# Attention scores of a diffusion backbone from rounded queries and keys: one float32 product becomes three

## The chip, the cores and the metric

The program runs on one core of a Trainium2 chip. The metric is the device time of one execution in microseconds (us), the median of several runs. TensorE multiplies matrices, VectorE and ScalarE work elementwise, GpSimd ("POOL" in the profile) helps, SyncE ("SP") issues most transfers. All five run their own instruction streams and meet through semaphores.

## What is computed

Two layers: windowed attention with grouped heads, rotary positions and a learned sink, then an mLSTM. The change touches the attention of the first layer alone, cut here to what matters:

```python
# 2048 latent tokens, 16 query heads, 4 key/value heads, head size 64, blocks of 128 queries
q = _axial_rope(q); k = _axial_rope(k)
def block(args):                       # 128 queries
    keys = concat([ck, kb])            # 256 cached keys and 384 in the window (256 at both ends)
    vals = concat([cv, vb])
    return _sink_attend(qblk, keys, vals, mask, sink)

def _sink_attend(q, k, v, mask, sink):
    s = einsum('bqhgd,bkhd->bhgqk', q, k) * HEAD_DIM ** -0.5
    s = where(mask, s, -inf)
    m = maximum(max(s), sink)
    p = exp(s - m)
    return einsum('bhgqk,bkhd->bqhgd', p, v) / (sum(p) + exp(sink - m))
```

All inputs are float32. 128 context tokens attend only to themselves.

## The kernel before

`phase_attn` (from L533) holds the attention layer. Every engine has one stream, written out by hand; its order is the order of the code, and nothing moves it.

**Heads.** The loop runs over four key/value heads `kv`. Each has five projections `m` of 128 columns: keys and values (`m=0`), two pairs of query heads (`m=1`, `m=3`) and their gates (`m=2`, `m=4`). The token axis of 2176 is cut into five groups `GROUPS` of 512, 512, 384, 384 and 384. A unit is one projection of one group: 24 matmuls, eight slices of the inner dimension by three products of rounded parts (`pe_slices`, L522 to L524): low weights by high activations, high by low, high by high. A rounded part has the type `fp32r`; the remainder is float32 minus the rounded part, rounded again.

**Weights.** For each projection SyncE loads the raw weights; ScalarE (`J.act_hi`, L501) or GpSimd (L491) rounds them in two halves, and VectorE (`J.dve_lo`, L507) makes the remainders. There is one buffer for each part, so the first half of the next projection's high weights waits until TensorE has used the first half for the last time, and the second half until the projection is finished. TensorE starts a projection when the first half of the low weights is there.

**Rotary.** For groups of keys and queries VectorE shuffles the columns out of PSUM (L823) into `shuf`, multiplies by the cosine (L826), GpSimd multiplies `shuf` by the sine (L721) and adds it (L726). For the keys ScalarE then copies rows 0 to 63 of `kT` to rows 64 to 127 (L745), since the two query heads of a pair lie in the two halves of `qT`.

**Softmax stage.** After the first three units of a gate projection come the blocks `b` of 128 queries, 16 latent and one of context, for two heads at once. On TensorE one step is `scores` of a block (L1000 against the 256 cached keys, L1002 against the window), `turn` of the block before (L1013, transposes of the probabilities) and `pv` of the one before that (L1025, and L1027 for the reciprocals). VectorE takes scale, mask and maximum in one instruction (L852), copies half of the turned probabilities (L866) and applies the gate (L881, L883); ScalarE does the exponentials (L790) and the other copies (L777, L780). Two heads' scores lie in four PSUM banks.

**Buffers.** `E.arena` (eight rows of 1024) holds raw and rounded weights in rows 0 to 2, the rotary tables `cs` in 3 and 4, both `shuf` in 5 and three of the four `prob` in 6 and 7. After the attention its first slices take `attn_w_out` for the next phase, `E.w_ahead` of them.

Of the kernel before, what the change touches and what calls it, by code (L numbers as in the profile page):

```python
# [28 lines left out]
P = 128  # L29
# [22 lines left out]
WMID, WFIRST = 0, 5 * P  # L52
# [5 lines left out]
FIRST_STAGE = 47 * D  # L58
# [31 lines left out]
def at(n):  # L90


    return n + 1
# [21 lines left out]
def first_stage(E, take, s_first_lo):  # L115
# [332 lines left out]
    S.s_lo, S.s_ha, S.s_hd, S.s_mod, S.s_grow = s_lo, s_ha, s_hd, s_mod, s_grow  # L448
# [89 lines left out]
def phase_attn(E):  # L538
    nc = E.nc
    SWAP = [(p + 16) % 32 for p in range(32)]  # L540
    with ExitStack() as ctx:
        sem = lambda n: E.semaphore(n)
        sb = Shelf(nc, E.attn_where)
        kT = sb("kT", [P, KCOLS])
        gT = sb("gT", [P, T])
        vS = sb("vS", [P, VTILES, HD])
        qT = sb("qT", [P, T])
        spare = E.arena
        cs = [spare[:, 3 + b, :].rearrange("p (a n) -> p a n", a=2) for b in range(2)]
        shuf = [spare[:, 5, b * 512:(b + 1) * 512] for b in range(2)]  # L550
        pair = spare[:, 6:8, :].rearrange("p a n -> p (a n)")
        prob = [pair[:, b * 640:(b + 1) * 640] for b in range(3)] + [sb("prob3", [P, 640])[:, :]]
        probT = [sb(f"probT{b}", [P, 2, 5, P]) for b in range(2)]
        gth = [probT[1][:, :, :, :].rearrange("p h t q -> p (h t q)")[:, e * 512:(e + 1) * 512] for e in range(2)]
        sb = Shelf(nc, E.attn_where + FIRST_STAGE)
# [3 lines left out]
        negm = sb("negm", [P, 2, 2])  # L559
        rsum = sb("rsum", [P, 2, 2])  # L560
        sarg = sb("sarg", [P, 2, 2])
        esink = sb("esink", [P, 2, 2])
        den = sb("den", [P, 2, 2])
        rden = sb("rden", [P, 2, 2])
        rspr = sb("rspr", [P, 2, 2, HD])
        kvout = sb("kvout", [P, 2, HD])
# [3 lines left out]
        s_wo = sem("w_out_loaded")  # L570
        (s_shuf, s_cos, s_rope, s_gth, s_release, s_kdup, s_vT, s_vS, s_kvo, s_kvst, s_ckl, s_cvl,
# [37 lines left out]

        weighted, spread = E.bank[6][:, 0:P], E.bank[6][:, P:2 * P]  # L610
# [16 lines left out]
        with nc.Block() as block:  # L627
            @block.sync
            def _(sp):
# [23 lines left out]
                for kv in range(NKV):  # L653
# [27 lines left out]
                    if last:  # L681
                        sp.wait_ge(J.s_unit, at(NKV * 5 * NG))
                        sp.wait_ge(s_rope, at(NKV * ROPES))
                        n_ahead = E.w_ahead
                        sp.dma_start(spare[:, 0:n_ahead, :], E.a["attn_w_out"][0].rearrange("(k p) m -> p k m", p=P)[:, 0:n_ahead, :]).then_inc(s_wo, 16)
# [7 lines left out]
                sp.wait_ge(s_wo, at(16))  # L693
# [1652 lines left out]
```

## Time and profile before

| | |
|---|---|
| median of 3 runs | 2811.59 us (2811.55 to 2812.96) |
| the profiled execution | 2810.98 us, span 2809.1 us |
| busy share of the span | PE 96%, PEld 82%, DVE 45%, ACT 29%, POOL 23% |
| mean granted TensorE clock | 0.989 |
| attention layer's projections and softmax stages | 116 to 1125 us of the span |

PE is TensorE's matmul, PEld its weight load, DVE VectorE, ACT ScalarE. Ends of matmul records are modelled, so they overlap; the time of a matmul is better read from one start to the next. A wait has the line that released it behind it.

### The profile page before, as it was taken

The numbers are of one execution on the slowest core, as the hardware profiler recorded it, in microseconds if no ns is written. First come the engines' busy times: TensorE is split into PE (matmuls) and PEld (weight loads), VectorE is DVE, ScalarE is ACT, GpSimd is POOL, SyncE is SP. The second block draws the span as 40 slices with busy tenths as digits, with TensorE's granted clock in tenths as the row PEclk, the third lists the DMA queues.
The fourth block names the chain that finished last, engine by engine and source line by source line (L and its number), as shares of the span: only waits on it lengthen the run. The fifth ranks groups of instructions, "written<-read, shape, count | busy, mean of one in ns | idle before, by whom it ended". The sixth has DMA issues, their size and how long they took to land.

```text
span 2809.1 us, 46819 instructions
## 1 busy us (share of the span) xinstructions
PE 2703.8 (96%) x16995; PEld 2312.8 (82%) x16995; DVE 1268.0 (45%) x3434; ACT 822.9 (29%) x2140; POOL 640.2 (23%) x792
## 2 busy tenths in 40 slices
PE   5899999999999999799999999999999999998998
PEld 3687787878788887588689999999999999998787
DVE  3645646464655547555324242333334241514533
ACT  3433525242443425122312222222313131312111
POOL 2511030103112110433103121221203040303532
PEclk9999999999999999899999999999999999999999
DMA  9511030102012011433113131122222020316343
GB/s 358 195 54 49 7 92 5 54 25 72 31 26 67 29 39 47 138 135 135 48 29 77 45 61 53 47 75 36 78 40 82 18 95 25 81 41 190 108 144 105
DMA packets 183958, 213.29 MB, mean 76 GB/s; under 512 B 26288, under 2 KB 131712, under 8 KB 181840
## 3 DMA queue, kind: packets, MB, share of 16 engines
q1 hardware_dynamic: 173776, 183.18, 22.4%
q10 hardware_dynamic: 9984, 27.37, 2.5%
q8 instruction: 137, 2.24, 0.3%
q14 instruction: 61, 0.50, 0.1%
HBM read 172.44 MB, written 38.07 MB: 75 GB/s over the span
## 4 chain that ended last, share of the span: by engine, by line
PE 56%; DVE 2%; DMA 1%; issue 1%; POOL 0%; SPq 0%; ACT 0%; DVEq 0%; POOLq 0%
PE psum L522 11%; PE psum L524 11%; PE psum L523 11%; PE psum L2145 2%; PE psum L1284 2%; PE psum L1286 2%; PE psum L1285 2%; PE psum L2209 2%; PE psum L1703 2%; PE psum L1704 2%; PE psum L1705 2%; PE psum L2212 2%; PE psum L2193 1%; PE psum L2136 1%; PE psum L2100 1%
## 5 line engine op out<-in xcount | busy, mean ns | idle before, releaser
L522 PE MATMUL psum<-h_hi,m_w_lo 128*128 128x384 f32 (+1 forms) x1600 | 605.0, 378 | 4.7 <-DVE m_w_lo L507 3.6
L524 PE MATMUL psum<-h_hi,m_w_hi 128*128 128x384 f32 (+1 forms) x1600 | 574.5, 359 | 0.0
L523 PE MATMUL psum<-h_lo,m_w_hi 128*128 128x384 f32 (+1 forms) x1600 | 573.7, 359 | 0.0
L522 PEld LDWEIGHTS psum<-h_hi,m_w_lo 128*128 128x128 f32 x1600 | 302.2, 189 | 27.7 <-issue 5.2
L524 PEld LDWEIGHTS psum<-h_hi,m_w_hi 128*128 128x128 f32 x1600 | 300.8, 188 | 27.3
L523 PEld LDWEIGHTS psum<-h_lo,m_w_hi 128*128 128x128 f32 x1600 | 302.5, 189 | 20.4
L522 PE MATMUL psum<-h_hi,attn_w_lo 128*128 128x384 f32 (+1 forms) x800 | 290.9, 364 | 1.2 <-DVE attn_w_lo L507 1.1
L524 PE MATMUL psum<-h_hi,attn_w_hi 128*128 128x384 f32 (+1 forms) x800 | 285.7, 357 | 0.0
L523 PE MATMUL psum<-h_lo,attn_w_hi 128*128 128x384 f32 (+1 forms) x800 | 285.4, 357 | 0.0
L790 ACT ACTIVATE arena<-arena,negm 128x640 f32<-128x640 f32 (+2 forms) x208 | 161.8, 778 | 201.2 <-DVE negm L852 201.2
L491 POOL CAST m_w_hi<-m_w_raw 128x512 fp32r<-128x512 f32 x80 | 50.0, 625 | 713.6 <-PE psum L524 651.0
L852 DVE CUSTOM_DVE_ANT_0 arena<-psum,wmask,nsk 128x640 f32<-128x640 f32 (+2 forms) x208 | 167.1, 826 | 59.0 <-PE psum L1002 54.5
L2043 DVE TENSOR_TENSOR m_gth<-psum,m_hc 128x256 f32<-128x256 f32 x136 | 51.7, 419 | 287.0 <-PE psum L2136 287.0
L1025 PE MATMUL psum<-probT,vS 128*64 128x128 f32 x2528 | 168.0, 278 | 6.7 <-DVE gT L883 6.4
L522 PEld LDWEIGHTS psum<-h_hi,attn_w_lo 128*128 128x128 f32 x800 | 150.9, 189 | 24.7 <-issue 12.2
L507 DVE TENSOR_TENSOR m_w_lo<-m_w_raw,m_w_hi 128x512 fp32r<-128x512 f32 x80 | 59.5, 746 | 234.5 <-POOL m_w_hi L491 234.5
L711 POOL COPY rspr<-rden 128x128 f32<-128x128 f32 x136 | 40.3, 296 | 540.4 <-DVE rden L876 540.4
L524 PEld LDWEIGHTS psum<-h_hi,attn_w_hi 128*128 128x128 f32 x800 | 150.2, 188 | 13.1
L1025 PEld LDWEIGHTS psum<-probT,vS 128*64 128x64 f32 x2528 | 135.5, 136 | 30.7 <-issue 30.7
L523 PEld LDWEIGHTS psum<-h_lo,attn_w_hi 128*128 128x128 f32 x800 | 150.3, 188 | 12.1
L1013 PEld LDWEIGHTS psum<-ident,arena 128*128 128x128 f32 x952 | 102.6, 141 | 68.9 <-issue 63.4
L1883 POOL TENSOR_TENSOR m_bc<-m_bc,m_causal 128x256 f32<-128x256 f32 x136 | 101.7, 748 | 247.1 <-DMA m_bc<-gate_rows_mlstm 242.1
(275 smaller groups left out, 4826.9 us busy)
## 6 DMA issues: line engine op xcount, KB each, us to landing
m_bc<-gate_rows_mlstm SPq DMA_DIRECT2D x128, 256.0 KB, 3.7
m_w_raw<-in_mlstm_w_in SPq DMA_DIRECT2D x40, 512.0 KB, 4.8
h_full<-gated_output SPq DMA_DIRECT2D x31, 512.0 KB, 3.8
gated_output<-gT SPq DMA_DIRECT2D x8, 1088.0 KB, 4.9
layer_output<-xb_out ACTq DMA_DIRECT2D x17, 512.0 KB, 2.6
h_hi_full<-layer_output SPq DMA_DIRECT2D x17, 512.0 KB, 4.7
out<-h_hi_full ACTq DMA_DIRECT2D x17, 512.0 KB, 4.8
xb<-in_x_sample ACTq DMA_DIRECT2D x16, 512.0 KB, 6.9
```

The lines of the kernel that those rows point to most:

```text
L507: dve.tensor_tensor(self.lo[:, k, :], self.raw[:, k, :], self.hi[:, k, :], ALU.subtract).then_inc(self.s_lo, 1)
L522: pe.matmul(out, self.lo[:, k, :], E.h_hi[:, k, tok], start=(k == 0), stop=False)
L523: pe.matmul(out, self.hi[:, k, :], E.h_lo[:, k, tok], start=False, stop=False)
L524: ins = pe.matmul(out, self.hi[:, k, :], E.h_hi[:, k, tok], start=False, stop=(k == KT - 1))
L790: act.activation(x, x, ACT.Exp, bias=negm[:, b % 2, hh:hh + 1], scale=-1.0, accum_out=rsum[:, b % 2, hh:hh + 1]).then_inc(s_p, 1)
L852: dve.tensor_tensor_reduce(prob[w % 4][:, 0:n], scores_of(w), E.wmask[:, m0:m0 + n], scale=-(HD ** -0.5), scalar=nsk[:, 2 * sub + hh:2 * s ...
L1013: ins = pe.transpose(out, prob[w % 4][:, t * P:(t + 1) * P], E.ident[:, :])
L1025: pe.matmul(weighted[HD * hh:HD * hh + HD, :], vS[:, v, :], probT[b % 2][:, hh, t, :], start=(t == 0), stop=(t == len(tiles) - 1))
L1284: pe.matmul(out, og_lo[j][:, k, :], w_hi[:, k, c], start=(k == 0), stop=False)
L1285: pe.matmul(out, og_hi[j][:, k, :], w_lo[:, k, c], start=False, stop=False)
L1286: ins = pe.matmul(out, og_hi[j][:, k, :], w_hi[:, k, c], start=False, stop=(k == KT - 1))
L1883: pool.tensor_tensor(bc[x][:, 0:2, :], bc[x][:, 0:2, :], E.causal[:, :, :], ALU.add).then_inc(s_E, 1)
```

## The change

The scores of latent blocks come from rounded parts `q_hi`, `k_hi` and remainders `q_lo`, `k_lo`: three products of type `fp32r` in place of one float32 product. ScalarE makes the high parts, VectorE the low ones; `k_lo` lies over `kT` and `q_lo` over `qT`, `q_hi` over the rotary tables. For this one shuffle buffer goes, all four `prob` move into the arena, the mask loses its second copy, `kvout` lies in `probT[0]`, and one slice less of `attn_w_out` is loaded ahead. The context block stays float32.

```diff
+        split = lambda name, at0, cols: nc.alloc_sbuf_tensor_at(name, [P, cols], F32R, offset=at0)
+        k_lo = split("k_lo", sb.at, KREQ)
         kT = sb("kT", [P, KCOLS])
...
+        q_lo = split("q_lo", sb.at, SAMPLE)
         qT = sb("qT", [P, T])
+        q_hi = split("q_hi", E.arena_at + 3 * 4 * D, SAMPLE)
...
-        shuf = [spare[:, 5, b * 512:(b + 1) * 512] for b in range(2)]
+        shuf = spare[:, 5, 0:512]
...
+        k_hi = sb("k_hi", [P, KREQ], F32R)
...
     def rotary(kv, m, g):
...
+                    if g == 0 and m != 1:
+                        sp.wait_ge(s_S, at(kv * (2 * NU) + (NU if m == 3 else 0)))
...
-                        sp.dma_start(spare[:, 0:n_ahead, :], ...)
+                        sp.dma_start(spare[:, 0:3, :], w_out[:, 0:3, :]).then_inc(s_wo, 16)
+                        sp.wait_ge(s_S, at(NKV * (2 * NU)))
+                        sp.dma_start(spare[:, 3:E.w_ahead, :], w_out[:, 3:E.w_ahead, :]).then_inc(s_wo, 16)
...
     ScalarE, keys, behind the copy to rows 64 to 127 of each group g:
+                        if kv == 0 and g == 0:
+                            act.wait_ge(S.s_gst, 32)
+                        act.wait_ge(s_kdup, at(kv * NG + g + 1))
+                        act.copy(k_hi[:, keys_part(g)], kT[:, keys_part(g)]).then_inc(s_khi, 1)
...
+                    act.wait_ge(s_ckl, at(kv * 16 + 16))
+                    act.copy(k_hi[:, keys_part(NG)], kT[:, keys_part(NG)]).then_inc(s_khi, 1)
...
     ScalarE, queries, ahead of the gates:
+                        act.wait_ge(s_rope, at(kv * ROPES + NG * (2 + sub)))
+                        for i in range(QPARTS):
+                            act.copy(q_hi[:, queries_part(i)], qT[:, queries_part(i)]).then_inc(s_qhi, 1)
...
     VectorE, rotary:
-                    dve.wait_ge(s_rope, at(kv * ROPES + (rope - 1 if rope >= 2 else 0)))
+                    dve.wait_ge(s_rope, at(kv * ROPES + rope))
...
+                        def keys_low(i):
+                            c = keys_part(i)
+                            dve.wait_ge(s_khi, at(kv * (NG + 1) + i + 1))
+                            dve.tensor_tensor(k_lo[:, c], kT[:, c], k_hi[:, c], ALU.subtract).then_inc(s_klo, 1)
...
                                 rope_unit(kv, rope, m, HD, kT, KLAT, KREQ, g)
                                 dve.tensor_copy(gT[HD:P, tok], unit_bank(m, g)[HD:P, 0:w]).then_inc(s_release, 1)
                                 rope += 1
+                                if g >= 2:
+                                    keys_low(g - 2)
...
+                                if m == 1 and g < 2:
+                                    keys_low(NG - 2 + g)
...
+                                if g == 0:
+                                    if m == 2:
+                                        keys_low(NG)
+                                    for i in range(QPARTS):
+                                        queries_low(i)
...
     TensorE, scores:
-                        for hh, r in enumerate(rows):
-                            pe.matmul(E.bank[2 * hh][:, 256:512], q[hh], kT[r, 0:PAST], start=True, stop=True)
...
+                        parts = ((q_lo, k_hi), (q_hi, k_lo), (q_hi, k_hi))
+                        for n, (x, y) in enumerate(parts):
+                            for hh, r in enumerate(rows):
+                                pe.matmul(E.bank[2 * hh][:, 256:512], x[r, t], y[r, 0:PAST], start=(n == 0), stop=(n == 2))
...
-                    pe.wait_ge(s_rope, at(kv * ROPES + NG * (2 + sub)))
+                    pe.wait_ge(s_qlo, at((kv * 2 + sub) * QPARTS + QPARTS))
...
-                E.w_low, E.w_ahead = cw.enter_context(nc.sbuf_tensor("w_low", [P, KT, D], F32R)), 6
+                E.w_low, E.w_ahead = cw.enter_context(nc.sbuf_tensor("w_low", [P, KT, D], F32R)), 5
```

VectorE's order in the key projection of one head, before, from the third group on. `attn_w_lo` is `J.dve_lo` for the first query projection, the shuffle of `64x256` belongs to the last group:

```order
L823 STREAM_SHUFFLE arena<-psum 64x384 [waits attn_unit_done,rotated]
L826 TENSOR_TENSOR kT<-psum,arena 64x384 [waits rotary_loaded0]
L896 COPY gT<-psum 64x384
L823 STREAM_SHUFFLE arena<-psum 64x384 [waits attn_unit_done,rotated]
L826 TENSOR_TENSOR kT<-psum,arena 64x384 [waits rotary_loaded1]
L896 COPY gT<-psum 64x384
L507 TENSOR_TENSOR attn_w_lo<-attn_w_raw,attn_w_hi 128x512 [waits attn_w_hi_ready] x2
L823 STREAM_SHUFFLE arena<-psum 64x256 [waits attn_unit_done,rotated]
```

And now, the same stretch:

```order
L854 STREAM_SHUFFLE arena<-psum 64x384 [waits attn_unit_done,rotated]
L857 TENSOR_TENSOR kT<-psum,arena 64x384 [waits rotary_loaded0]
L941 COPY gT<-psum 64x384
L923 TENSOR_TENSOR k_lo<-kT,k_hi 128x512 [waits keys_hi]
L854 STREAM_SHUFFLE arena<-psum 64x384 [waits attn_unit_done,rotated]
L857 TENSOR_TENSOR kT<-psum,arena 64x384 [waits rotary_loaded1]
L941 COPY gT<-psum 64x384
L923 TENSOR_TENSOR k_lo<-kT,k_hi 128x512 [waits keys_hi]
L506 TENSOR_TENSOR attn_w_lo<-attn_w_raw,attn_w_hi 128x512 [waits attn_w_hi_ready] x2
L854 STREAM_SHUFFLE arena<-psum 64x256 [waits attn_unit_done,rotated]
```

Two subtractions of keys, each with a wait for `keys_hi`, now stand ahead of the low weights.

ScalarE in the same projection, before. The two casts are the halves of `J.act_hi` for the first query projection:

```order
L501 CAST attn_w_hi<-attn_w_raw 128x512 [waits attn_w_first_half_used,attn_w_loaded]
L501 CAST attn_w_hi<-attn_w_raw 128x512 [waits attn_unit_done]
L745 COPY kT<-kT 64x512 [waits rotated] x2
L745 COPY kT<-kT 64x384 [waits rotated] x2
L745 COPY kT<-kT 64x256 [waits proj_bank_free,rotated]
```

And now:

```order
L500 CAST attn_w_hi<-attn_w_raw 128x512 [waits attn_w_first_half_used,attn_w_loaded]
L500 CAST attn_w_hi<-attn_w_raw 128x512 [waits attn_unit_done]
L765 COPY kT<-kT 64x512 [waits rotated]
L773 CAST k_hi<-kT 128x512 [waits k_doubled,gate_rows_stored]
L765 COPY kT<-kT 64x512 [waits rotated]
L773 CAST k_hi<-kT 128x512 [waits k_doubled]
L765 COPY kT<-kT 64x384 [waits rotated]
```

Each copy is followed by a cast of the same group, and all of them stay behind both weight halves.

TensorE in one step of the softmax stage, from the scores of a block to the first transposes of the block before. Before:

```order
L1000 MATMUL psum<-kT,qT 128x256 [waits neg_max]
L1000 MATMUL psum<-kT,qT 128x256
L1002 MATMUL psum<-kT,qT 128x384 x2
L1013 MATMUL psum<-ident,arena 128x128 [waits probs,probsT_second_ready,probsT_first_ready]
L1013 MATMUL psum<-ident,arena 128x128 x4
```

And now:

```order
L1057 MATMUL psum<-k_hi,q_lo 128x256 [waits neg_max]
L1057 MATMUL psum<-k_hi,q_lo 128x256
L1057 MATMUL psum<-k_lo,q_hi 128x256 x2
L1057 MATMUL psum<-k_hi,q_hi 128x256 x2
L1060 MATMUL psum<-k_hi,q_lo 128x384 x2
L1060 MATMUL psum<-k_lo,q_hi 128x384 x2
L1060 MATMUL psum<-k_hi,q_hi 128x384 x2
L1073 MATMUL psum<-ident,arena 128x128 [waits probs,probsT_second_ready,probsT_first_ready]
```

Four products have become twelve; the rest of the step is the same.

## Rows read from the trace of the kernel before

**Rows 1.** Waits of TensorE from 116 to 1125 us: in total, times, longest.

```profile
PE psum L1025 <- DVE gT L883: 6.4, 8, 0.8
```

**Rows 2.** Timeline of TensorE, one softmax step and beyond: start, duration, instruction, count.

```profile
204.66 0.70 PE L1000 MATMUL psum<-kT,qT 64*128 64x256 f32 x4
...
208.68 0.70 PE L1000 MATMUL psum<-kT,qT 64*128 64x256 f32 x4
...
209.96 1.31 PE L1013 MATMUL psum<-ident,arena 128*128 128x128 f32 x10
211.20 1.31 PE L1025 MATMUL psum<-probT,vS 128*64 128x128 f32 x20
...
214.60 0.74 PE L1013 MATMUL psum<-ident,arena 128*128 128x128 f32 x5 [0.49 <-issue]
```

**Rows 3.** One step as a window: length, then busy PE, PEld, DVE, ACT, POOL.

```profile
204.76:208.78 4.02, 4.02 (x41) 2.97 (x41) 3.28 (x10) 2.56 (x9) 0.30 (x1) 1.00 0.00 0
```

**Rows 4.** Timeline of TensorE, float32 products of 129 columns on the full array.

```profile
1703.62 0.38 PE L2209 MATMUL psum<-m_v,m_bc 128*128 128x129 f32 x2
1703.84 0.39 PE L2212 MATMUL psum<-m_states,m_bc 128*128 128x129 f32 x2
```

**Rows 5.** Timeline of TensorE, projection products of rounded numbers, 512 and 384 columns.

```profile
502.05 0.39 PE L522 MATMUL psum<-h_hi,attn_w_lo 128*128 128x512 f32 x1
...
502.73 0.39 PE L522 MATMUL psum<-h_hi,attn_w_lo 128*128 128x512 f32 x1
...
515.33 0.33 PE L522 MATMUL psum<-h_hi,attn_w_lo 128*128 128x384 f32 x1
...
515.85 0.35 PE L522 MATMUL psum<-h_hi,attn_w_lo 128*128 128x384 f32 x1
```

**Rows 6.** Timelines of TensorE, ScalarE and VectorE, end of the second key projection.

```profile
389.34 0.47 PE L522 MATMUL psum<-h_hi,attn_w_lo 128*128 128x512 f32 x1 [0.51 <-DVE attn_w_lo L507]
388.86 0.62 ACT L501 CAST attn_w_hi<-attn_w_raw 128x512 fp32r<-128x512 f32 x1 [1.41 <-PE psum L524]
389.50 1.97 ACT L745 COPY kT<-kT 64x512 f32<-64x512 f32 x4
388.11 1.08 DVE L507 TENSOR_TENSOR attn_w_lo<-attn_w_raw,attn_w_hi 128x512 fp32r<-128x512 f32 x1
```

**Rows 7.** The same engines at the end of the first key projection.

```profile
136.39 0.47 PE L522 MATMUL psum<-h_hi,attn_w_lo 128*128 128x512 f32 x1
137.07 1.97 ACT L745 COPY kT<-kT 64x512 f32<-64x512 f32 x4
132.44 0.59 DVE L823 STREAM_SHUFFLE arena<-psum 64x384 f32<-64x384 f32 x1
...
133.49 0.56 DVE L896 COPY gT<-psum 64x384 f32<-64x384 f32 x1
```

**Rows 8.** TensorE behind a wait, timeline, and a window (granted clock, then DMA last).

```profile
1403.54 0.47 PE L522 MATMUL psum<-h_hi,m_w_lo 128*128 128x512 f32 x1 [3.59 <-DVE m_w_lo L507]
...
1404.80 0.63 PE L524 MATMUL psum<-h_hi,m_w_hi 128*128 128x512 f32 x1
...
1407.79 0.56 PE L522 MATMUL psum<-h_hi,m_w_lo 128*128 128x512 f32 x1
1406.00:1408.00 2.00, 2.00 (x6) 1.54 (x5) 0.00 (x0) 0.00 (x0) 0.00 (x0) 0.50 0.70 208
```

**Rows 9.** Rotary of a full query group (VectorE, GpSimd) and its loads' landing.

```profile
262.87 0.74 DVE L823 STREAM_SHUFFLE arena<-psum 128x512 f32<-128x512 f32 x1
265.69 1.29 POOL L726 TENSOR_TENSOR qT<-qT,arena 128x512 f32<-128x512 f32 x1
arena<-in_rotary SPq DMA_DIRECT2D x16, 512.0 KB, 5.2
```

**Rows 10.** Timeline of VectorE at the start of the next phase.

```profile
1138.47 11.93 DVE L1248 TENSOR_TENSOR w_low<-arena,w_hi_out 128x1024 fp32r<-128x1024 f32 x6
```

**Rows 11.** The start of the program as a window; GB/s stand last.

```profile
0.00:98.00 98.00, 63.96 (x470) 40.04 (x471) 43.88 (x106) 42.64 (x100) 30.44 (x31) 0.97 1.02 365
```

More of the change, by code:

```diff
@@ L558, in phase_attn @@
         nsk = sb("nsk", [P, 4])
[L559 to L564, printed above, removed]
+        stats = sb("stats", [P, 6, 2, 2])
+        negm, rsum, sarg, esink, den, rden = (stats[:, x, :, :] for x in range(6))
         rspr = sb("rspr", [P, 2, 2, HD])
-        kvout = sb("kvout", [P, 2, HD])
+        kvout = probT[0][:, 0, 0, :].rearrange("p (a d) -> p a d", a=2)
         J = Projection(E, ctx, "attn", 5, E.first_w)
@@ L608, in scores_of, with window, keys_part @@
             return pair[:, first:first + width(w // 2)]
+        def window(b):
+            if b == 0:
+                return bass.AP(tensor=E.wmask[:, :].tensor, offset=0, ap=[[MASK, P], [3 * P, 2], [1, 2 * P]])
+            return E.wmask[:, 0:width(b)]
+        def keys_part(i):
+            if i == NG:
+                return slice(0, PAST)
+            t0, wl, wc = lat_ctx(i)
+            return slice(KLAT + t0, KLAT + t0 + wl)
+        queries_part = lambda i: slice(i * 512, i * 512 + 512)
+        QPARTS = SAMPLE // 512
         weighted, spread = E.bank[6][:, 0:P], E.bank[6][:, P:2 * P]
@@ L864, in turned_first @@
                             dve.wait_ge(s_pv, at(bbase + (b - 1 if b >= 2 else 0)))
+                            if b == 0 and sub == 0:
+                                dve.wait_ge(s_kvst, at(kv * 32 + 32))
                             n = min(4, len(value_tiles(b)))
@@ L998, in scores @@
                         k0, k1 = KLAT + max(b - 1, 0) * P, KLAT + min(b + 2, NS) * P
-                        for hh, r in enumerate(rows):
-                            pe.matmul(E.bank[2 * hh][:, 256:512], q[hh], kT[r, 0:PAST], start=True, stop=True)
-                        for hh, r in enumerate(rows):
-                            pe.matmul(E.bank[2 * hh + 1][:, 0:k1 - k0], q[hh], kT[r, k0:k1],
-                                      start=True, stop=True).then_inc(s_S, 1)
+                        t = slice(b * P, (b + 1) * P)
+                        parts = ((q_lo, k_hi), (q_hi, k_lo), (q_hi, k_hi))
+                        for n, (x, y) in enumerate(parts):
+                            for hh, r in enumerate(rows):
+                                pe.matmul(E.bank[2 * hh][:, 256:512], x[r, t], y[r, 0:PAST], start=(n == 0), stop=(n == 2))
+                        for n, (x, y) in enumerate(parts):
+                            for hh, r in enumerate(rows):
+                                ins = pe.matmul(E.bank[2 * hh + 1][:, 0:k1 - k0], x[r, t], y[r, k0:k1],
+                                                start=(n == 0), stop=(n == 2))
+                                if n == 2:
+                                    ins.then_inc(s_S, 1)
                     def turn(b):
@@ L2318, in shape_constants @@
     own = np.zeros((P, P), f)
-    window = np.concatenate([own, own, prev, own, nxt] + [own, own, own, nxt], 1)
+    window = np.concatenate([own, own, prev, own, nxt], 1)
     causal = np.stack([np.where(q <= j, 0, BIG), np.where(q >= j, 0, BIG)], 1).astype(f)
```

42 lines of the change are left out of this document (24 added, 18 removed).

## The prediction

> **What bounds the kernel now.** I read the page first: TensorE is busy for 96% of the span. Busy says little where matmuls are pipelined, so the next view was TensorE's list of waits over the attention layer, 116 to 1125 us. Its longest entry is 6.4 us in a thousand [rows 1]. In this layer, then, everything that shortens TensorE's own stream is a gain, unless another engine then comes last, and everything that makes TensorE wait is a loss with nothing beside it. All terms below lie in this layer; its eight softmax stages (four key/value heads, two subs each) hold 16 latent blocks each, 128 in all.
>
> The timeline of one block [rows 2] shows the period: scores from 208.68 to 209.96 (1.28 us), turning the probabilities 1.24, the value products and the spread of the reciprocals behind them for the rest of 4.02 us (the scores of the block before start at 204.66), with no idle time between them. VectorE works for 3.28 us in such a stretch of 4.02 [rows 3]; ScalarE for 2.56.
>
> **The score products, the gain.** A score block before is four float32 products (two heads by 256 and by 384 columns), each two records. Do the two heads, in rows 0 to 63 and 64 to 127, run side by side? A float32 product of 129 columns on the full array takes two records and 0.22 us, 1.7 ns a column [rows 4]. The block's 1280 columns would be 2.2 us one after the other; they take 1.28 [rows 2]. So the heads overlap: 640 columns by 1.7 ns are 1.09 us and about 0.2 us is filling and changing over.
>
> After it there are twelve products of rounded numbers, six pairs of heads. The projections show such products on all 128 rows: three take 0.52 us at 384 columns and 0.68 at 512 [rows 5], so 0.173 and 0.227 each, and 0.120 at 256 on the same line. If a pair overlaps as the float32 pairs do, the block is 3 x 0.120 + 3 x 0.173 + 0.2 = 1.08 us, 0.2 less. 112 full blocks by 0.2 are 22.4 us; the 16 blocks at either end of the sequence have 256 columns in place of 384 and give about 0.13, 2.1 us. Sum 24.5 us. The bounds: a column costs (0.227 - 0.173) / 128 = 0.42 ns, so a projection product pays 13 ns beyond its columns, and a float32 record (0.110 us for 129 columns at twice that) only 2 or 3. If a pair pays 3 ns, the sum is 32 us; if each of its two products pays 13 of its own, 15 us. I take the pair at 13, since the projections are the only rows with this type.
>
> A rule of the Trainium skill speaks on this. The row first: twenty records of the value products lie within 1.31 us, 65 ns for one [rows 2]. The skill ("TensorE: Matmul & The Clock Gate", section "Wait — 56ns, not 53.3ns?") states about 62 ns of the sequencer for each matmul where decoding is not done in hardware. By that rule an estimate for twelve matmuls is 0.74 us, below the 1.08 of the sum, and a 256-column pair would be 0.124 us instead of 0.120, so that the gain would be 1.5 us smaller.
>
> The block now ends 0.2 us sooner, and the 0.74 us in which VectorE has nothing shrink to 0.54: TensorE still comes last. Once a stage VectorE also splits weights, and TensorE then waits 0.49 us, at 214.60 [rows 2]; with 0.2 less slack that wait grows by 0.2 in seven stages, 1.4 us lost.
>
> **The splits of the keys, the loss.** The roundings are new on ScalarE, the remainders new on VectorE. Their places decide. VectorE has `keys_low(0)` right behind the third key group and `keys_low(1)` behind the fourth, both ahead of `J.dve_lo`, which makes the low weights of the first query projection; the order excerpt in the change section shows it. `keys_low(0)` waits for ScalarE's first `k_hi`. ScalarE has that behind `J.act_hi`, whose second half waits until the key projection is finished on TensorE. TensorE wants the low weights at that very moment. So a ring of four engines' work stands on the path, at each of the four key/value heads.
>
> Before, for the second of them [rows 6]: TensorE starts the next projection at 389.34, the low weights (started at 388.11, 1.08 us) being just done; ScalarE's second cast starts at 388.86, the key copies at 389.50. After, from 389.50: copy about 0.62 with its completion, cast to `k_hi` 0.62 (as the cast of a weight half, the same 128x512 elements), 390.8; `keys_low(0)` some 0.7 with nobody beside it, 391.5; the fourth group's shuffle, cosine product and copy, 1.61 from 132.44 to 134.05 in the first head [rows 7], 393.2; `keys_low(1)` and the first half of `J.dve_lo` beside a busy GpSimd, 1.08 each as in the row at 388.11, 395.4; TensorE's first product 0.15 later, 395.55. That is 6.2 us later than 389.34. For the first head the same chain starts at ScalarE's copies at 137.07 and TensorE had started at 136.39 [rows 7], 6.7 us. Sum 3 x 6.2 + 6.7 = 25.3 us. With 0.7 for the two contended steps it is 22.
>
> Such a wait also lowers TensorE's clock. After one of 3.59 us the 512-column products go from 0.23 apart to 0.43 between 1404.80 and 1407.79 [rows 8], seven products 2.99 us apart in all, 1.4 us lost; the window row has a granted clock of 0.50 there, the 1.2 GHz level. The waits here are longer, so I take 3.8 us at half clock, 1.9 us lost, four times 7.6 us; bounds 0 and 10.
>
> What hides the rest. The query splits (four casts of 0.62 and four subtractions) come 15 us before `scores(0)` needs them: three projection units lie between. The single shuffle buffer puts shuffle, cosine and both GpSimd products in a row: from the shuffle at 262.87 to the end of the last at 266.98 [rows 9], 4.1 us, a little under the 4.2 us of the shortest full projection unit; without that cover every group would pay the difference. The first two rotary loads of a projection now wait for a stage's last scores; a load lands in 5.2 us [rows 9], and a whole projection unit of 24 products, 5.4 us, and the last blocks' turning and value products lie over it; without them it would be 5 us each time, seven times. Behind these loads on SyncE stand only the store of `gT`, which waits for later work anyway. Of `attn_w_out` one more slice is left to the next phase; VectorE needs 2.0 us for each of the slices ahead of it [rows 10], and the load is wanted after five of them. Nothing. The mask is 256 KB smaller in a start that moves 365 GB/s [rows 11], 0.7 us; bound 0; I take 0.5.
>
> **Sum.** -24.5 + 1.4 - 0.5 + 25.3 + 7.6 = +9.3 us. On the profiled execution's 2811.0 this is 2820.3; the median of the runs is 0.6 above it, so 2820.5.
>
> **The rivals.** (a) Not slower: a pair of rounded products costs its columns and 3 ns. The gain is 32 us and with a stall of 22 + 7.6 the time is 2811 - 32 + 1.4 - 0.5 + 29.6 = 2809.5. It decides from a score block of about 1.0 us down. For it: the float32 records carry so little. Against: the projections' products of this type carry 13. (b) Faster: the ring does not close, because the first `k_hi` is ready when VectorE comes (it would have to be before the key projection ends). Then only the gain is left, 2811 - 23.6 = 2787. Program order speaks against it. (c) The rounded products of two heads do not overlap: six pairs take 2 x (0.35 + 0.52) = 1.75 + 0.2, 0.67 us more than before, 128 times, about +80 instead of -24.5: 2925; if only their weight loads come one after the other, about 0.2 more, 2870. No row shows 64-row products of this type. (d) VectorE becomes the bound of the softmax stage and the period stays 4.02: no gain, 2844. Against it stand its 3.28 us.
>
> **Chances.** Forecast 0.58 (2808 to 2832); (a) 0.15; (b) 0.08; (c) 0.10; (d) 0.09. The range 2805 to 2843 takes in (a) in most of its width and (d) in part, and leaves out (b) and (c). A measurement here tells 0.2% (5.6 us) from no change. Slower: 0.58 x 0.8 + 0.10 + 0.09 = 0.65; within: 0.10 + 0.11 = 0.21; faster: 0.08, 0.05 of (a) and a rest, 0.14.
>
> **What would show it.** The gain: score blocks of 1.07 us and a period near 3.8 in the timeline. The loss: in TensorE's waits four of about 6 us before the first query projection, released by the low weights, and before them VectorE waiting some 4 us for `k_hi`; granted clock 0.50 for 3 to 5 us behind each. Wrong would make it: score blocks above 1.28 us, no such waits, or waits at `scores(0)` or for rotary loads.

## The result, and the profile after

The changed kernel takes 2827.2 us, the median of five runs (2823.6 to 2828.0), beside 2812.4 us for the kernel before on the same chip: ratio 1.0053, 95% interval 1.0042 to 1.0064. It is 14.8 us slower. The forecast was 2820.5 us. The profiled execution took 2827.6 us with a span of 2825.8, against 2811.0 and 2809.1 of the one before.

I laid the starts of the same places in both traces side by side. The table gives how much later than before the changed kernel is; it was +14.8 us in the medians and is +16.7 at the end of TensorE's work in these two traces.

| place in the program | after minus before |
|---|---|
| first projection product | -1.5 us |
| first scores of key heads 1 to 4 | +6.8, +11.6, +15.9, +19.8 |
| last scores of a head's second softmax stage | +2.4, +7.5, +11.7, +15.3 |
| end of the attention layer | +15.3 |
| last product of the program | +16.7 |

So each key projection loses time (8.3, 9.2, 8.4 and 8.1 us, 34.1 together), and each head's two softmax stages give some back (4.4, 4.1, 4.2 and 4.6 us, 17.3 together).

**The gain.** TensorE in two steps of the softmax, to be read against [rows 2] (start, duration, instruction, count):

```profile
206.92 0.38 PE L1057 MATMUL psum<-k_hi,q_lo 64*128 64x256 f32 x2
207.14 0.28 PE L1057 MATMUL psum<-k_lo,q_hi 64*128 64x256 f32 x2
207.26 0.28 PE L1057 MATMUL psum<-k_hi,q_hi 64*128 64x256 f32 x2
207.38 0.34 PE L1060 MATMUL psum<-k_hi,q_lo 64*128 64x384 f32 x2
207.56 0.34 PE L1060 MATMUL psum<-k_lo,q_hi 64*128 64x384 f32 x2
207.73 0.34 PE L1060 MATMUL psum<-k_hi,q_hi 64*128 64x384 f32 x2
208.06 1.28 PE L1073 MATMUL psum<-ident,arena 128*128 128x128 f32 x10
...
210.78 0.39 PE L1057 MATMUL psum<-k_hi,q_lo 64*128 64x256 f32 x2
...
214.60 0.38 PE L1057 MATMUL psum<-k_hi,q_lo 64*128 64x256 f32 x2
```

The starts tell more than the durations, since matmuls are pipelined. The first pair of 256 columns takes 0.22 us up to the next pair; from then on a pair of 256 columns takes 0.12 and a pair of 384 takes 0.17 to 0.18, as the sum had them. From the first score product to the first transpose it is 1.14 and 1.10 us in turn where it was 1.28, and 3.86 or 3.82 to the next block where it was 4.02: 0.18 us a step.

The same step as a window, to be read against [rows 3] (length, busy PE, PEld, DVE, ACT, POOL, granted clock, DMA share, GB/s):

```profile
206.92:210.78 3.86, 3.86 (x45) 3.12 (x45) 3.32 (x11) 2.60 (x9) 0.29 (x1) 1.00 0.01 4
```

TensorE is still without idle time; VectorE has about 0.5 us left of the 0.74 it had.

**The loss.** Waits of TensorE in the attention layer (total, times, longest):

```profile
PE psum L521 <- DVE attn_w_lo L506: 27.9, 4, 7.0
PE psum L1073 <- issue: 7.6, 17, 0.7
PE psum L1085 <- DVE gT L918: 7.0, 9, 0.8
```

The first line is four waits of 7.0 us, one for each key head. The kernel before had at the same place, in all four heads together:

```profile
PE psum L522 <- DVE attn_w_lo L507: 1.1, 3, 0.5
```

The end of the second key projection in the timelines of ScalarE, VectorE and TensorE, to be read against [rows 6]:

```profile
391.12 0.62 ACT L500 CAST attn_w_hi<-attn_w_raw 128x512 fp32r<-128x512 f32 x1 [1.41 <-PE psum L523]
391.76 0.62 ACT L765 COPY kT<-kT 64x512 f32<-64x512 f32 x1
392.40 0.62 ACT L773 CAST k_hi<-kT 128x512 fp32r<-128x512 f32 x1
...
393.06 0.69 DVE L923 TENSOR_TENSOR k_lo<-kT,k_hi 128x512 fp32r<-128x512 f32 x1 [4.11 <-ACT k_hi L773]
...
393.78 0.58 DVE L854 STREAM_SHUFFLE arena<-psum 64x384 f32<-64x384 f32 x1
...
395.42 1.06 DVE L923 TENSOR_TENSOR k_lo<-kT,k_hi 128x512 fp32r<-128x512 f32 x1
...
396.40 2.08 DVE L506 TENSOR_TENSOR attn_w_lo<-attn_w_raw,attn_w_hi 128x512 fp32r<-128x512 f32 x2
...
398.02 0.76 PE L521 MATMUL psum<-h_hi,attn_w_lo 128*128 128x512 f32 x1 [6.95 <-DVE attn_w_lo L506]
```

It is the ring of the forecast, link by link: the second weight half on ScalarE, copy, `k_hi`; VectorE, which had waited 4.11 us for it; the remainder, the fourth group's rotary unit, the next remainder, the low weights; TensorE. The two halves of the low weights, which share the row at 396.40, are not alike (number, then shortest, median and longest in ns, first and last start):

```profile
L506 DVE TENSOR_TENSOR attn_w_lo<-attn_w_raw,attn_w_hi x2: 678/1076/1475, 396.4 to 397.8; 128x512 fp32r<-128x512 f32 x2
```

The first half, for which TensorE waits, takes 1.48 us beside GpSimd's work (396.40 to 397.88), the second 0.68 without it. TensorE starts 0.14 us behind the first. Behind the wait stands the slower clock (the columns of the step's window):

```profile
398.00:401.00 3.00, 2.98 (x7) 2.42 (x8) 2.55 (x7) 0.41 (x1) 1.51 (x2) 0.50 0.54 173
401.00:404.40 3.40, 3.40 (x9) 2.59 (x9) 0.00 (x0) 1.01 (x3) 0.21 (x1) 0.53 0.38 91
404.40:408.00 3.60, 3.60 (x17) 3.00 (x16) 1.20 (x3) 0.00 (x0) 0.00 (x0) 1.00 0.70 214
```

The granted clock is 0.50 and 0.53, so for 6.3 us TensorE runs at the 1.2 GHz level; before the fall it had waited 7.0 us. Taking the starts of the 512-column products against the 0.227 us that they are apart otherwise, it loses 2.9 us there, and 1.5, 2.1 and 1.5 in the first, third and fourth head, 8.0 together.

### The profile page after: what moved, and what is told of

Read it like the earlier page. It is cut to its first block, busy times and chain, and to the rows that moved or that the text cites. A ratio compares the mean times of both kernels' runs of the same rounds, so it can differ in the third digit from the quotient of the medians.

```text
span 2825.8 us, 47969 instructions
## 1 busy us (share of the span) xinstructions
PE 2690.1 (95%) x17507; PEld 2336.0 (83%) x17507; DVE 1299.8 (46%) x3490; ACT 852.2 (30%) x2196; POOL 644.0 (23%) x792
## 4 chain that ended last, share of the span: by engine, by line
PE 55%; DVE 2%; issue 1%; DMA 1%; POOL 0%; ACT 0%; SPq 0%; DVEq 0%; POOLq 0%
PE psum L521 11%; PE psum L523 11%; PE psum L522 11%; PE psum L1344 2%; PE psum L1346 2%; PE psum L1345 2%; PE psum L2205 2%; PE psum L2269 2%; PE psum L1763 2%; PE psum L1764 2%; PE psum L1765 2%; PE psum L2272 2%; PE psum L2253 1%; PE psum L2196 1%; PE psum L2160 1%
## 5 line engine op out<-in xcount | busy, mean ns | idle before, releaser
L521 PE MATMUL psum<-h_hi,attn_w_lo 128*128 128x384 f32 (+1 forms) x800 | 294.4, 368 | 28.2 <-DVE attn_w_lo L506 27.9
L818 ACT ACTIVATE arena<-arena,stats 128x640 f32<-128x640 f32 (+2 forms) x272 | 213.0, 784 | 184.5 <-DVE stats L885 184.5
L885 DVE CUSTOM_DVE_ANT_0 arena<-psum,wmask,nsk 128x640 f32<-128x640 f32 (+2 forms) x256 | 206.2, 840 | 37.8 <-PE psum L1060 33.7
L1085 PE MATMUL psum<-probT,vS 128*64 128x128 f32 x2528 | 168.0, 278 | 7.0 <-DVE gT L918 7.0
L1073 PE MATMUL psum<-ident,arena 128*128 128x128 f32 x1264 | 164.2, 276 | 10.3 <-issue 7.6
L1073 PEld LDWEIGHTS psum<-ident,arena 128*128 128x128 f32 x1264 | 136.9, 141 | 42.7 <-issue 38.0
L506 DVE TENSOR_TENSOR m_w_lo<-m_w_raw,m_w_hi 128x512 fp32r<-128x512 f32 x80 | 59.5, 746 | 234.8 <-POOL m_w_hi L490 234.8
L1085 PEld LDWEIGHTS psum<-probT,vS 128*64 128x64 f32 x2528 | 135.5, 136 | 31.0 <-issue 31.0
L731 POOL COPY rspr<-stats 128x128 f32<-128x128 f32 x136 | 39.9, 293 | 524.6 <-DVE stats L911 524.6
```

Of the source, the lines that this page charges most:

```text
L506: dve.tensor_tensor(self.lo[:, k, :], self.raw[:, k, :], self.hi[:, k, :], ALU.subtract).then_inc(self.s_lo, 1)
L521: pe.matmul(out, self.lo[:, k, :], E.h_hi[:, k, tok], start=(k == 0), stop=False)
L818: act.activation(x, x, ACT.Exp, bias=negm[:, b % 2, hh:hh + 1], scale=-1.0, accum_out=rsum[:, b % 2, hh:hh + 1]).then_inc(s_p, 1)
L885: dve.tensor_tensor_reduce(x, y, window(b), scale=-(HD ** -0.5), scalar=nsk[:, 2 * sub + hh:2 * sub + hh + 1], op0=ALU.add, op1=ALU.min, a ...
L1073: ins = pe.transpose(out, prob[w % 4][:, t * P:(t + 1) * P], E.ident[:, :])
L1085: pe.matmul(weighted[HD * hh:HD * hh + HD, :], vS[:, v, :], probT[b % 2][:, hh, t, :], start=(t == 0), stop=(t == len(tiles) - 1))
```

## The experiments

The theory was: the ring, closed by the order of VectorE and ScalarE, costs all of the 34 us; TensorE is last in the softmax step, so the score products' 0.18 us a step arrive in full. The rivals: it is the amount of added work, not its place; the one shuffle buffer; a limit other than TensorE in the softmax step. The kernels ran in three groups, each on one chip with the kernel before among them; its medians were 2811.3 (experiments 1, 2, 5 and 7), 2812.4 (3, 4, 8 and the first of 9) and 2812.2 us (6 and the second of 9).

**1. The remainders of the keys moved behind the key projection.**

```diff
-                                if g >= 2:
-                                    keys_low(g - 2)
...
-                                if m == 1 and g < 2:
-                                    keys_low(NG - 2 + g)
+                                if m == 1:
+                                    keys_low(g)
```

> One edit to the changed kernel: VectorE writes the remainders of the keys after the first query projection's rotary units, one group behind each, instead of three of them within the key projection. Casts, remainders and score products are all the same. Theory of the ring (VectorE's k_lo waits for ScalarE's k_hi, which is queued behind the weight copy that waits for the key projection's end, and the low weights are queued behind that k_lo): the four waits of 7.0 us at L521 (27.9 us) fall to what they were before (0.5 to 3.6 us), the clock of 0.50 behind them goes too. The four key heads cost 8.3, 9.2, 8.4 and 8.1 us over the kernel before, 34 us together, so 2827 - 34 = 2793 us, between 2789 and 2799. Rival one: it is the amount of added work on VectorE and ScalarE, not its place. Then the remainders, 4 us a head, come up again ahead of the first query's rotary units or of the first scores, and less than 10 us is gained: 2817 us or more. Rival two: the score products are what costs: no change, 2827 us.

Measured: 2805.9 us, ratio to before 0.9981 (0.9972 to 0.9990). It lies between my theory and rival one. The first head lost its stall wholly. Heads two to four kept waits of 2.7 to 2.9 us, with a slower clock behind them that cost nothing in the second head, 1.5 us in the third and 2.9 in the fourth. All of TensorE's waits for these weights, then VectorE in the second head:

```profile
PE psum L521 <- DVE attn_w_lo L506: 9.8, 7, 2.9
```

```profile
369.84 0.01 DVE L854 LOAD_MASK_SELECT arena<-psum  x1 [5.28 <-DMA gated_output<-gT]
...
374.10 0.01 DVE L854 LOAD_MASK_SELECT arena<-psum  x1 [2.21 <-issue]
...
378.36 0.01 DVE L854 LOAD_MASK_SELECT arena<-psum  x1 [2.20 <-issue]
...
381.78 0.01 DVE L854 LOAD_MASK_SELECT arena<-psum  x1 [1.78 <-issue]
...
383.45 2.48 DVE L506 TENSOR_TENSOR attn_w_lo<-attn_w_raw,attn_w_hi 128x512 fp32r<-128x512 f32 x2
```

The first of these rows waits for the store of the gated output, so VectorE begins the head late, at 369.8; TensorE has been at this projection since 355. The rows behind it say "issue", but in the program a shuffle waits there until GpSimd has finished the group before, and each row starts 0.14 or 0.15 us behind the end of GpSimd's addition. So the units come 4.26 us apart (3.4 behind a group of 384), and the low weights come late. This points at a second cause, the one shuffle buffer.

**2. ScalarE's casts of two groups ahead of its weight copy.**

```diff
-                    J.act_hi(act, kv * 5 + 1, kv * 6 + 3)
                     for g in range(NG):
+                        if g == 2:
+                            J.act_hi(act, kv * 5 + 1, kv * 6 + 3)
```

> One edit to the changed kernel, on ScalarE alone: the copy of the keys to the second half of the rows and their cast to k_hi stand ahead of the copy of the next weights for the first two groups, behind it for the other three. VectorE's order stays as it was, with the remainders within the key projection. Theory of the ring: a ring opens at either link, so the four waits of 7.0 us go here as well, and the time comes to that of the kernel with late remainders within 2 us, 2791 to 2797 us. Rival one (VectorE's order alone is at fault, its remainders take 1.5 us of the projection's last unit whatever ScalarE does): half of the 34 us or less returns, 2810 us or more. Rival two (the casts ahead delay the weight copy, since they wait for the rotary sums of GpSimd): waits of 1 to 2 us stay at L521, 2800 us.

Measured: 2812.9 us, 1.0003 (0.9993 to 1.0012) of before, and 14.3 less than the changed kernel. Waits of 1.2 us in the first head and of 4.5 to 4.6 in each of the others stayed:

```profile
PE psum L521 <- DVE attn_w_lo L506: 14.8, 4, 4.6
```

My theory (2791 to 2797) missed by 16 us, and by the number it is rival one, VectorE's order. The ring is opened at this link too, since the waits fell, but more is left than with late remainders; experiment 6 takes it apart.

**3. Two shuffle buffers alone, and 4. with late remainders.**

```diff
-        shuf = spare[:, 5, 0:512]
+        shuf = [spare[:, 5, b * 512:(b + 1) * 512] for b in range(2)]
...
-                    dve.wait_ge(s_rope, at(kv * ROPES + rope))
+                    dve.wait_ge(s_rope, at(kv * ROPES + (rope - 1 if rope >= 2 else 0)))
```

> The changed kernel with two shuffle buffers again, nothing else. Two causes may share the stall: the ring over k_hi, and the one shuffle buffer, by which VectorE shuffles a group only when GpSimd has finished the group before (4.25 us from one shuffle to the next in the later heads, while 2.1 us were seen with two buffers where VectorE had a backlog). Theory (the ring is closed by its order alone; the buffer adds nothing while it is closed, since its links, 6 us from the end of the projection, start only then): the four waits stay at 7 us and the time at 2827, within 2 us. Rival (the buffer is the cause of the stall): what late remainders left, 2.4 us of gap in three heads and their clock, comes off here too: 12 us, 2815 us.

> The kernel with late remainders and with two shuffle buffers. With late remainders alone the first key head lost its stall wholly, but heads two to four kept waits of 2.8 to 3.0 us (0.5 us in the kernel before) and, behind them, 0, 1.5 and 3.0 us of slower clock: about 7.5 + 4.5 = 12 us. Theory (VectorE comes to these three heads with a backlog, and one buffer lets it work off only one group in 4.2 us): all of it goes, the waits fall to 0.5 us, 2806 - 12 = 2794 us, 2790 to 2798. Rival one (the waits are the cost of the casts k_hi that stand on ScalarE ahead of or between its weight copies): at most 3 us return, 2803 us or more. Rival two (the stall goes, but VectorE or ScalarE is late at the next place, the query's casts ahead of the first scores): 2798 to 2803 us, with new waits there.

Measured: alone 2828.2 us, no less than the changed kernel's 2827.2, with the same four waits:

```profile
PE psum L521 <- DVE attn_w_lo L506: 27.9, 4, 7.0
```

With late remainders 2793.4 us, 0.9934 (0.9921 to 0.9948) of before, 12.5 less than with one buffer. TensorE's waits in the attention layer of the latter:

```profile
PE psum L1071 <- issue: 7.6, 17, 0.7
PE psum L1083 <- DVE gT L918: 7.0, 9, 0.8
PE psum L521 <- DVE attn_w_lo L506: 2.2, 7, 0.3
```

The second head's units now start at 370.4, 372.4, 374.6 and 379.1 us, and the granted clock stays at 1.00 through all four places where it had fallen. Both theories held. The two causes lie behind one another: the buffer costs 12.5 us when the ring is open and nothing when it is closed, because the ring's links start only when the projection has ended. The whole is 2827.2 - 2793.4 = 33.8 us, beside the loss of 34.1 read from the two traces.

**5. Program order of the heads.**

```diff
-                        for n, (x, y) in enumerate(parts):
-                            for hh, r in enumerate(rows):
+                        for hh, r in enumerate(rows):
+                            for n, (x, y) in enumerate(parts):
```

> The kernel with late remainders, and the score products in another order: the three of one head in a row and then the three of the other, where the changed kernel alternates between the heads, whose rows are the lower and the upper 64 of TensorE. The same twelve products. Theory (products on different rows run side by side: two of 256 columns in 0.12 us and two of 384 in 0.175 us, which is what one alone would need at 0.42 ns a column, 0.11 and 0.16 us): in a row they don't, a full block goes from 6 x 0.15 to 12 x 0.15 us on average, +0.88 us, and as TensorE is the last in the period, 112 full blocks bring +99 us and 16 at the edges about +10: 2793 + 109 = 2902 us, 2880 to 2920. Rival (the rounded products are fast whatever their rows; the accumulation into two banks in turn is what costs nothing): the block stays at 1.1 us and the time at 2793 us.

Measured: 2806.9 us beside 2805.9 for the same kernel with alternating heads; no difference, and 95 us from what my theory expected. TensorE's timeline:

```profile
206.86 0.39 PE L1055 MATMUL psum<-k_hi,q_lo 64*128 64x256 f32 x2
207.08 0.29 PE L1055 MATMUL psum<-k_lo,q_hi 64*128 64x256 f32 x2
207.20 0.29 PE L1055 MATMUL psum<-k_hi,q_hi 64*128 64x256 f32 x2
207.32 0.35 PE L1058 MATMUL psum<-k_hi,q_lo 64*128 64x384 f32 x2
```

The program has one head's three products ahead of the other's first, and still each runs beside its fellow on the other 64 rows. So this could not tell what products without overlap cost. It tells that they overlap in either order, over a distance of three.

**6. The ring opened at ScalarE's link, two buffers.** Both edits, of 2 and of 3.

> The kernel with ScalarE's casts of the first two groups ahead of its weight copy, with VectorE's remainders where the changed kernel has them, inside the key projection, and with two shuffle buffers. With one buffer it came to 2813 us, and kept waits of 4.6 us in heads two to four, 1.2 in the first. Theory (there the ring was open, and the one buffer did the rest): with two buffers the waits fall to 0.5 us and the time to that of late remainders with two buffers, 2793 us, 2791 to 2797. Rival (two remainders of 1.06 us each still stand ahead of the low weights on VectorE, at the end of the projection, where it is itself the last): waits of 1 to 2 us stay, with a slower clock behind some, 2797 to 2804 us.

Measured: 2801.8 us, 0.9957 (0.9942 to 0.9972); the rival won. TensorE waits 2.1 us in each of heads two to four, and 0.3 in the first. Its waits, then VectorE in the second head:

```profile
PE psum L521 <- DVE attn_w_lo L506: 6.7, 4, 2.1
```

```profile
382.79 0.55 DVE L858 TENSOR_TENSOR kT<-psum,arena 64x384 f32<-64x384 f32 x1 [2.69 <-DMA arena<-in_rotary]
...
383.96 1.07 DVE L924 TENSOR_TENSOR k_lo<-kT,k_hi 128x512 fp32r<-128x512 f32 x1
...
386.73 1.08 DVE L924 TENSOR_TENSOR k_lo<-kT,k_hi 128x512 fp32r<-128x512 f32 x1
387.73 2.08 DVE L506 TENSOR_TENSOR attn_w_lo<-attn_w_raw,attn_w_hi 128x512 fp32r<-128x512 f32 x2
```

No wait stands ahead of either remainder, but the two take 1.07 and 1.08 us at a place where VectorE is itself last. That is the size of the 2.1 us. VectorE is last there because it is late: it waited 5.25 us for the store of the gated output and, in the row shown, 2.69 us for the third group's rotary table. The kernel before has both of these waits too (5.36 and 2.64 us); in the first head it has no store to wait for, and there the remainders cost next to nothing. The 6.7 us of waits, less the 2.2 of the kernel of experiment 4, and 0, 1.6 and 1.7 us of slower clock behind them are 7.8 us; measured are 8.4 over that kernel. So the stall has a third part: work in the wrong place costs its own duration where its engine is behind, even with no ring. The second buffer brought 11.1 us here (2812.9 to 2801.8) and 12.5 with late remainders.

**7. One product instead of three.** With late remainders; the two products with the remainders are left out, and the scores have the precision of rounded numbers.

```diff
-                        parts = ((q_lo, k_hi), (q_hi, k_lo), (q_hi, k_hi))
+                        parts = ((q_hi, k_hi),)
```

> The kernel with late remainders, and of the three score products only rounded query by rounded key is left; the two with the remainders are left out, so the scores have the precision of rounded numbers. All casts and remainders are still made. A block loses 2 pairs of 256 columns (0.24 us) and 2 of 384 (0.35 us), 0.59 us. Theory (TensorE sets the period, with 0.39 us of VectorE idle in each): the period falls from 3.84 by 0.39 to 0.45 us until VectorE sets it, 112 x 0.4 = 45 us and some 5 at the edges: 2793 - 50 = 2743 us, 2730 to 2755. Rival one (TensorE bound all through, VectorE's idle time is no measure): the full 0.59 us, 2793 - 70 = 2723 us. Rival two (VectorE or the chain of semaphores through both is the bound already, which is why only 2.0 of the 2.9 us per stage came): less than 15 us, 2780 us or more.

**8. Four products.** With late remainders and two buffers.

```diff
-                        parts = ((q_lo, k_hi), (q_hi, k_lo), (q_hi, k_hi))
+                        parts = ((q_lo, k_lo), (q_lo, k_hi), (q_hi, k_lo), (q_hi, k_hi))
```

> The kernel with late remainders and two shuffle buffers, and a fourth product, remainder of the query by remainder of the key, ahead of the other three: one more pair of 256 columns (0.12 us) and one of 384 (0.175 us), 0.295 us a full block. It asks whether TensorE is the last in the period at three products. Theory (it is): the period grows from 3.84 by the full 0.29 to 4.13 us, 112 x 0.29 = 33 us. With one product instead of three the period came only 0.12 us shorter, so below three products something else, the chain from scores over maximum and exponential to the transposes, is last. Rival (that chain is last at three products too, and covers a part): the period grows by 0.15 us or less, 17 us in all.

Measured: one product 2786.4 us, only 19.5 below the same kernel with three, where my theory expected 50; it is nearest to rival two. Four products 2826.7 us in one profiled execution, 33.3 above the same kernel with three, where I expected 33. First TensorE with one product (and a row of VectorE), then with four:

```profile
197.86 0.39 PE L1055 MATMUL psum<-k_hi,q_hi 64*128 64x256 f32 x2
...
199.15 1.28 PE L1071 MATMUL psum<-ident,arena 128*128 128x128 f32 x10 [0.73 <-issue]
...
201.86 0.39 PE L1055 MATMUL psum<-k_hi,q_hi 64*128 64x256 f32 x2
...
202.57 1.28 PE L1071 MATMUL psum<-ident,arena 128*128 128x128 f32 x10 [0.15 <-issue]
...
205.29 0.39 PE L1055 MATMUL psum<-k_hi,q_hi 64*128 64x256 f32 x2
201.97 0.29 DVE L916 SCALAR_TENSOR_TENSOR gT<-psum,gT 128x128 f32<-128x128 f32 x1 [0.48 <-PE psum L1085]
```

```profile
207.84 0.39 PE L1055 MATMUL psum<-k_lo,q_lo 64*128 64x256 f32 x2
208.06 0.28 PE L1055 MATMUL psum<-k_hi,q_lo 64*128 64x256 f32 x2
208.18 0.28 PE L1055 MATMUL psum<-k_lo,q_hi 64*128 64x256 f32 x2
...
211.97 0.38 PE L1055 MATMUL psum<-k_lo,q_lo 64*128 64x256 f32 x2
```

With four the step is 4.13 us, 0.29 more, all of the added pairs (0.12 + 0.17). So in the steady step TensorE is last at three products, fully. The total is in part a lucky hit: 4.4 of the 33.3 us lie ahead of the first projection product (113.8 us against 109.4), which the edit does not touch, and 28.5 in the attention layer, since a few steps of a stage hardly grew. With one product it waits 0.73 and 0.15 us in turn ahead of the transposes, which need ScalarE's exponentials, and the steps last 4.00 and 3.43 us in turn, 3.72 on average instead of 3.84. Other engines' work forms a floor there, 0.12 us under the present step, not the 0.4 us that VectorE's idle time suggested. VectorE is part of it: it works through the shorter step without a wait, and in the longer one it waits 0.48 us for TensorE's product L1085, which stands behind the late transposes. Why the two kinds alternate is not shown.

**9. The next weights' remainders in slices, after and before.** With late remainders and two buffers, and then the kernel before with this edit alone.

```diff
-                            if s == 6 and not (last and m == 4):
-                                J.dve_lo(dve, kv * 5 + m + 1)
+                            if 6 <= s < 6 + KT and not (last and m == 4):
+                                J.dve_lo_slice(dve, kv * 5 + m + 1, s - 6)
```

`dve_lo_slice` subtracts one of the eight slices of 128 columns, with the wait ahead of each half's first and the signal behind its last.

> The kernel with late remainders and two shuffle buffers, and the remainders of the next weights, which VectorE computes as two halves in one step of the softmax, are computed in eight slices, one in each of eight steps. In the changed kernel that one step lasts 4.78 us where its neighbours last 3.84: 0.94 us in each of 7 stages. Theory (VectorE has 0.39 us idle in each step, TensorE is last, and a slice of 128 columns takes some 0.2 to 0.25 us): the step falls to 3.84 and the others stay, 7 x 0.94 = 6.6 us less than the same kernel without it, 2788 us, 2785 to 2791. Rival (the chain through VectorE has less slack than its idle time says: each slice adds 0.1 us or more to its step): 8 x 7 x 0.1 = 5.6 us come back, 2794 us.

> The kernel before, with one edit: the remainders of the next weights in eight slices over eight steps of the softmax, as in the kernel that has late remainders, two buffers and slices (2788 us). The scores stay in float32. It tells how much of that kernel's gain belongs to the change at all. In the kernel before, the step with both halves lasts 4.62 us against 4.02 of its neighbours, 0.60 us in each of 7 stages. Theory (TensorE is last in each step, with 0.58 us of VectorE idle): 7 x 0.60 = 4.2 us less than before, 2808 us, 2806 to 2810; of the 25 us between the kernel before and the best one, 4 are then the slices' and 20 the score products'. Rival (the slices cost the other steps as much, or the ratio of 4 us drowns): 2812 us.

Measured: 2787.6 us, 0.9910 (0.9895 to 0.9925), and 2808.5 us, 0.9985 (0.9976 to 0.9994). Both theories held. A slice in VectorE's timeline of the former, with the start of the next maximum:

```profile
212.07 0.28 DVE L512 TENSOR_TENSOR attn_w_lo<-attn_w_raw,attn_w_hi 128x128 fp32r<-128x128 f32 x1
...
212.80 0.88 DVE L892 CUSTOM_DVE_ANT_0 arena<-psum,wmask,nsk 128x640 f32<-128x640 f32 x1 [0.18 <-PE psum L1065]
```

0.18 us of idle time are left behind the slice, still released by TensorE, and of the full steps behind a stage's first only one in the eight stages is longer than 3.86 us (4.16). This kernel is the best of all that ran, 24.7 us under the kernel before. Against the kernel before with the same slices, the medians differ by 20.8 us. In the two traces 17.7 us of that lie in the attention layer, from its first product to its end, so the score products bring about 18 us there once their stall is gone; the rest is not told apart from the scatter of the other parts.

## Why the prediction was right, and where it was off

The direction and the mechanism were right, the time 6.7 us too low. By its steps:

- **Stall in the key projection**, +25.3 us: right. 27.9 us of waits, less the 1.1 us that TensorE waited there before, are 26.8. The chain was met link by link; in the second head the wait is 6.95 us, where the sum had 6.2 beyond one of 0.5. Of the two contended steps, taken at 1.08 us each, the second remainder took 1.06 but the first half of the low weights 1.48: that one was 0.4 us too small, and it is most of what the term lacks.
- **Clock behind it**, +7.6: right, 8.0 us, but in pieces of 1.5 to 2.9 us where the sum had four of 1.9. The two together, taken out by experiment 4, are 33.8 us; the sum had 32.9.
- **Score blocks**, -24.5, and **VectorE's slack**, +1.4, together -23.1: this is the term that was mis-sized; it measured -17.3, and the 5.8 us between the two are most of the 6.7. Pair spacings were met (0.12 and 0.17 to 0.18). Two things were not. The block came to 1.10 to 1.15 us instead of 1.08: the sum had 0.2 us for filling and changing over, and they are 0.10 at the first pair (0.22 instead of 0.12) and 0.12 to 0.16 behind the last (0.29 to 0.34 instead of 0.17). And the step count: of a stage's 14 steps (counted from one product L1087 to the next) only 10 became shorter by 0.16 to 0.21, 0.18 on average. The first (4.09 before, 4.13 after) lasts 4.12 or 4.13 with one, three and four products alike, so up to three products the scores are not what sets it; the one before last hardly moved (3.85 to 3.83); the step with the low weights grew from 4.62 to 4.78, where I had let the shorter block and the longer wait cancel: TensorE's waits in it, 0.49 before, became 0.69 and 0.15. I had multiplied one steady step by all 112 blocks.
- **Single shuffle buffer**, hidden: right for this kernel (experiment 3), but not for the reason given. I compared two rates, 4.1 us of chain against 4.2 us of projection. That holds only if VectorE starts level with TensorE, and in heads two to four it starts late: in experiment 1 at 369.8, where the first unit was done at about 360.5 (an estimate: the projection's start at 355.1 and 24 products of 0.227 us). The closed ring was what hid the buffer; with the ring open it costs 11.1 to 12.5 us.
- **Mask**, -0.5: not told apart. The first projection product started between 108.8 and 114.2 us in all the profiled executions, with no order by mask size. The rest of the 16.7 us, 1.2 after the attention layer, is likewise within the scatter of that part (1675.3 to 1678.0 us from the layer's end to the last product, over all twelve kernels).
- **Query splits, rotary loads, `w_out` slice**, hidden: right; no wait of TensorE names them.

Rival (a) asked for a block of about 1.0 us: it is 1.10 to 1.15. Rival (b)'s price, 2787, is nearly what the ring's opening gave (2793), with the missing 6 us in the score term. Rival (c), no overlap, asked for a block of 1.95 us and is refuted. Rival (d) is not the case, though closer than its 3.28 us of busy time said: the floor lies 0.12 us under the step.

The Trainium skill's figure of the sequencer, in the page "TensorE: Matmul & The Clock Gate", section "Wait — 56ns, not 53.3ns?", which the prediction weighed, gives an estimate of 0.124 us for a pair of 256 columns. The starts are 0.12 apart, and the sum's own price, worked out from the projections' rows, was 0.120. No run here tells the two apart.

## What to carry to other kernels

When a change adds steps to an in-order engine, ask for each what it waits for and what stands behind it; here a ring through two queues cost its whole length in each head, while the same work one projection later cost next to nothing (2.2 us of waits for the low weights against 1.1 before). When a stall has two causes in a row, removing one shows only what the other leaves, and removing the second alone may show nothing: do both before ruling either out. Price a gain per step by walking through every kind of step of a stage, the first, the last and the odd one, and read a floor from a run that takes the work away, not from another engine's idle time.

## What the runs showed of the hardware

- Products on rows 0 to 63 and on 64 to 127 run side by side even when the program has three of one half ahead of the first of the other (experiment 5: both heads' first products started within 0.01 us of each other, and neither the step nor the time changed). The Trainium skill, "TensorE: Matmul & The Clock Gate", section "🔬 Part 3: Packing small matmuls — row/col tiling", says that products on different row groups are concurrent, with which the trace agrees, and also that matmuls start and end strictly in program order. By that second rule the second head's first product could not start before the first head's third, at 207.20; both started by 206.87. The measurement decides against it.
- The clock behind a wait is not a function of the wait's length. In experiment 1 three waits of 2.7 to 2.9 us were followed by 0, 1.5 and 2.9 us of loss; in the changed kernel four waits of 7.0 us by 1.5, 2.9, 2.1 and 1.5. In the changed kernel with two buffers the same four waits were followed by 1.9, 1.6, 2.9 and 1.9.
- VectorE's remainder of 128x512 elements takes 0.68 to 0.69 us with GpSimd idle, and 1.06 (L923 above) and 1.48 us (L506) beside its rotary products; two that share one row of a timeline can be as unlike as 1.48 and 0.68.
